# A three-layer float32 transformer kernel: order of the opening loads, the first normalisation, and the experts' scatter

## The reference, cut to what matters

```python
sc, scc = silu(c), silu(c_ctx)[None]
mod_x = (sc @ w_mod + b_mod).reshape(-1, 6, d)         # shift, scale, gate, shift, scale, gate
mod_c = (scc @ w_mod[:, :2 * d] + b_mod[:2 * d]).reshape(1, 2, d)
hx = rms_norm(x, g_mix) * (1 + mod_x[:, 1]) + mod_x[:, 0]
hc = rms_norm(ctx, g_mix) * (1 + mod_c[:, 1]) + mod_c[:, 0]
mx = hybrid_mixer(hx, hc, w_in, ...)                   # projections, retention, two attentions
x = x + mod_x[:, 2] * mx
h = rms_norm(x, g_ffn) * (1 + mod_x[:, 4]) + mod_x[:, 3]
# experts: each of 16 takes its 32 best tokens
aff = softmax(h @ w_router)
gate, idx = top_k(swapaxes(aff, 1, 2), 32)
xe = h[idx]
hid = silu(xe @ w_gate[e]) * (xe @ w_up[e])
ye = (hid @ w_down[e]) * gate[..., None]
x = x + mod_x[:, 5] * zeros_like(h).at[idx].add(ye)
# second block: layer 0 a sparse attention and an FFN, layer 1 a recurrent mixer and an FFN
```

## Time and profile before

| | us |
|---|---|
| median of three runs | 1835.61 (1831.35 to 1838.48) |
| profiled execution, its time | 1840.93 |
| its span in the trace | 1839.1 |
| busy in the span: TensorE / VectorE / ScalarE / GpSimd | 1531.6 / 783.6 / 579.6 / 20.5 |
| moved by DMA | 437.75 MB, mean 238 GB/s |

### The profile page before, as it was taken

One profiled execution on the slowest core, in us unless ns is written; L12 is line 12 of the kernel. 1 busy time (PEld: TensorE's weight loads), 2 busy tenths in 40 slices (PEclk: granted clock), 3 DMA queues, 4 the chain that ended last, 5 costly groups with the idle time before them and its releaser, 6 DMA issues.

```text
span 1839.1 us, 27187 instructions
## 1 busy us (share of the span) xinstructions
PE 1531.6 (83%) x11234; PEld 1153.2 (63%) x11234; DVE 783.6 (43%) x1178; ACT 579.6 (32%) x832; POOL 20.5 (1%) x21
## 2 busy tenths in 40 slices
PE   5899996789976566666666799988999989879999
PEld 1689884467952111111111699547999989779999
DVE  4333335356741000000001566544655366765553
ACT  3322124466321000000001332454433344733332
POOL 0000020000000000000000000000000000100000
PEclk9899998889968766767666898889999999889999
DMA  9665454512638999999999453663355535335540
GB/s 395 250 252 213 194 184 181 208 69 93 249 140 367 421 422 422 421 422 422 422 422 422 159 201 115 267 256 118 138 183 184 184 138 184 133 115 183 183 168 24
DMA packets 60417, 437.75 MB, mean 238 GB/s; under 512 B 6720, under 2 KB 6848, under 8 KB 7456
## 3 DMA queue, kind: packets, MB, share of 16 engines
q1 hardware_dynamic: 59328, 428.89, 59.8%
q10 hardware_dynamic: 720, 4.94, 0.6%
q0 software_dynamic: 272, 2.49, 0.4%
HBM read 435.25 MB, written 1.05 MB: 237 GB/s over the span
## 4 chain that ended last, share of the span: by engine, by line
PE 59%; DMA 20%; DVE 10%; SPq 4%; ACT 4%; issue 3%; DVEq 0%; ACTq 0%
PE bank L631 55%; DMA ring<-in_w 20%; SPq L551 4%; DVE ring_r L1566 2%; PE bank L635 2%; PE bank L972 1%; PE bank L951 1%; ACT ring_r L1264 1%; DVE arena L1863 1%; DVE norm_t L1529 1%; DVE arena L1985 0%; DVE arena L1687 0%; ACT arena L1413 0%; DVE H L1556 0%; DVE arena L1986 0%
## 5 line engine op out<-in xcount | busy, mean ns | idle before, releaser
L631 PE MATMUL bank<-H_r,ring_r 128*128 128x256 f32 x3488 | 509.9, 288 | 18.5 <-DVE H_r L1551 18.5
L631 PEld LDWEIGHTS bank<-H_r,ring_r 128*128 128x128 f32 x3488 | 464.5, 196 | 24.2 <-issue 22.6
L1566 DVE TENSOR_TENSOR ring_r<-ring,ring_r 128x2048 fp32r<-128x2048 f32 x136 | 313.7, 2308 | 239.5 <-ACT ring_r L1264 239.3
L631 PE MATMUL bank<-arena_r,ring_r 128*128 128x256 f32 x2776 | 396.7, 287 | 20.5 <-DVE ring_r L1566 16.6
L631 PEld LDWEIGHTS bank<-arena_r,ring_r 128*128 128x128 f32 x2776 | 368.4, 194 | 37.5 <-issue 21.4
L1264 ACT ACTIVATE ring_r<-ring 128x2048 fp32r<-128x2048 f32 x136 | 259.6, 1910 | 229.3 <-PE bank L631 164.6
L951 PE MATMUL bank<-ring,arena 128*32 128x512 f32 x1024 | 195.7, 857 | 112.3 <-DMA ring<-in_w 111.8
L951 PEld LDWEIGHTS bank<-ring,arena 128*32 128x32 f32 x1024 | 24.3, 126 | 267.3 <-DMA ring<-in_w 260.2
L1819 DVE TENSOR_TENSOR arena<-arena,bank 64x512 f32<-64x512 f32 x16 | 11.1, 691 | 290.9 <-ACT arena L1361 290.9
L1361 ACT ACTIVATE arena<-bank 64x512 f32<-64x512 f32 x16 | 9.4, 588 | 385.6 <-PE bank L951 385.6
L631 PE MATMUL bank<-ring,silu_c 128*32 128x512 f32 x576 | 81.3, 670 | 47.1 <-ACT norm_t L1355 21.6
(11 more groups left out here) (238 smaller groups left out, 1275.7 us busy)
## 6 DMA issues: line engine op xcount, KB each, us to landing
ring<-in_w SPq DMA_DIRECT2D x408, 1024.0 KB, 10.6
ring<-in_bias POOLq DMA_DIRECT2D x1, 2048.0 KB, 7.7
consts<-in_consts ACTq DMA_DIRECT2D x1, 1567.0 KB, 25.1
X<-in_x ACTq DMA_DIRECT2D x1, 1024.0 KB, 10.7
arena<-in_ctx ACTq DMA_DIRECT2D x1, 1024.0 KB, 15.2
arena<-in_decay ACTq DMA_DIRECT2D x1, 1024.0 KB, 19.7
out_t<-X SPq DMA_DIRECT2D x4, 256.0 KB, 2.0
wide<-in_wide POOLq DMA_DIRECT2D x1, 256.0 KB, 9.0
```

The lines of the kernel that those rows point to most:

```text
L631: i = nc.tensor.matmul(o, lhsT, rhs, start=start, stop=stop, skip_group_check=grouped)
L1566: v.tensor_tensor(r(lo), lo, r(hi), ALU.subtract).then_inc(lo_ready, 1)
```

## The change

- The loads of x and ctx move to the head of SyncE's queue, before the chunks. ScalarE's queue keeps cols and the first 256 columns of consts (`ident`, `ones`). The rest of consts, decay and `wide` are started by GpSimd after modulation block 0 is done.
- x's sum of squares comes before the first modulation chunk, ctx's (`sum_sq_c`) after the second; each then has its own square root and reciprocal, and VectorE multiplies x and ctx by their inverse norms at once (one 128x2048 instruction each).
- FILL_START is gone: the seven steps stay in the fill list. ("kr", 0)'s chunk is loaded seventh, before the last two of block 0, and is split before the row copy.
- Apply 0 is made of three parallel parts: ScalarE makes the rounded part with gain and shift in one instruction, GpSimd makes the full part, VectorE subtracts. All of x's tiles go first, then ctx's.
- The decay masks are made head by head between the projections ("decay_m", h).
- The experts' loop on TensorE is written out for 16 experts. The picks' weighting and transposes go into expert 0. The combine is cut into four `scatter` groups: experts 0 to 3 are accumulated into banks 3 to 6 after the gate and up products of expert 4, and so on; the last group is behind expert 15.

The core of the diff:

```diff
-    s = [("decay",)] + [("mod", 0, k) for k in range(5)] + [("sum_sq", 0)]
-    s += [("mod", 0, k) for k in range(5, KT)] + [("mod_row", 0), ("mod_out", 0)]
+    s = [("decay",), ("sum_sq", 0), ("mod", 0, 0), ("mod", 0, 1), ("sum_sq_c",)]
+    s += [("mod", 0, k) for k in range(2, KT)] + [("mod_row", 0), ("mod_out", 0)]
...
-    take(FILL_START)
-    for x in [("kr", 0), ("kr", 1), ("qr", 0), ("qr", 1), ("vr", 0), ("rot", "kr", 0), ("vr", 1), ("rot", "kr", 1),
+    for x in [("kr", 0), ("kr", 1), ("decay_m", 0), ("qr", 0), ("decay_m", 1), ("qr", 1), ("decay_m", 2),
+              ("vr", 0), ("rot", "kr", 0), ("decay_m", 3), ("vr", 1), ("rot", "kr", 1), ("decay_m", 4),
...
-    s += [("gather", k) for k in range(KT)] + [("pick_t", t) for t in range(2)]
+    s += [("gather", k) for k in range(KT)]
     s += [("experts",)]
...
+        if x[0] == "mod" and x[1] == 0 and x[2] == LATE_MOD:
+            keys.append(("kr", 0))
+        if x[0] in ONE_CHUNK and x != ("kr", 0):
             keys.append(x)
...
-        x = mine[1 - n] if len(mine) >= n - 1 else ("apply", 0) if c < FIRST_SECOND else ("sum_sq", 2)
+        x = mine[1 - n] if len(mine) >= n - 1 else ("mod_row", 0) if c < FIRST_SECOND else ("sum_sq", 2)
...
+            for t in range(2):
+                add(("pick_t", t), "act", SUM_BANK + 2 * t)
+            for p in range(4):
+                add(("combine", p), "dve", SUM_BANK + p)
...
+            sp_eng.dma_start(X[:, :, :], small["x"]).then_inc(x_landed, 16)
+            sp_eng.dma_start(ctx_in, small["ctx"]).then_inc(ctx_landed, 16)
             for c, s in enumerate(RING_USE[0][1]):
                 load(s, w[c])
             rounds(0)
...
+            eng.wait_ge(mod_done, 1)
+            eng.dma_start(consts[:, 256:], small["consts"][:, 256:]).then_inc(rest_landed, 16)
+            eng.dma_start(decay_in, small["decay"]).then_inc(decay_landed, 16)
             eng.dma_start(wide[:, :, :], small["wide"]).then_inc(wide_landed, 16)
+
+            eng.wait_ge(x_hat, 2)
+            eng.wait_ge(mod_a_ready, 2)
+            for c in range(2):
+                for k in range(KT):
+                    nc.gpsimd.tensor_scalar(h_0[:, k, c * T:(c + 1) * T], H[:, k, c * T:(c + 1) * T],
+                                            mod_a[:, 2 * c, k:k + 1], mod[:, k, c:c + 1], ALU.mult,
+                                            ALU.add).then_inc(h_scaled, 1)
 
...
-                            pe.wait_ge(h_split, 2 * k + 1 + c)
+                            pe.wait_ge(h_split, KT * c + k + 1)
...
-                owed[0] += 1
+                if blk or k < LATE_MOD:
+                    owed[0] += 1
...
+            def scatter(i):
+
+                pe.wait_ge(ye_taken, 4 * i + 5)
+                if i == 0:
+                    in_sbuf(("pick_t", 1))
+                for p in range(4):
+                    b = begin(("combine", p)) if i == 0 else bank[SUM_BANK + p]
+                    for half in range(2):
+                        n = 2 * p + half
+                        mm(b[:, half * T:(half + 1) * T], y_tok[:, i, n * P:(n + 1) * P], hot_t[:, i, :],
+                           i == 0 and half == 0, i == 3, job_done if i == 3 and half else None, grouped=True)
...
+                for e in range(EXPERTS):
+
+                    pe.wait_ge(x_cur_ready, e + 1)
+                    for k in range(KT):
+                        c = FIRST_EXPERT + 12 * e + k
+                        pe.wait_ge(landed[slot_of(c)], 16 * landed_count(c))
+                        for j in range(4):
+                            last = matmul(bank[0][32 * j:32 * j + 32, :], x_cur[:, k, :],
+                                          ring[:, k, 512 * j:512 * j + 512], start=k == 0, stop=k == KT - 1)
+                        last.then_inc(chunk_used if k < KT - 1 else gate_up_done, 1)
+
+                    if e == 0:
+                        turn_picks()
+                    if e and e % 4 == 0:
+                        scatter(e // 4 - 1)
+
+                    pe.wait_ge(hid_ready, e + 1)
...
+                    last.then_inc(down_done, 1)
+
+                    pe.wait_ge(down_done, e + 1)
+                    pe.sem_inc(chunk_used, 1)
+                scatter(3)
...
-            act.dma_start(X[:, :, :], small["x"]).then_inc(x_landed, 16)
-            act.dma_start(ctx_in, small["ctx"]).then_inc(ctx_landed, 16)
-            act.dma_start(decay_in, small["decay"]).then_inc(decay_landed, 16)
-            act.dma_start(consts[:, :], small["consts"]).then_inc(consts_landed, 16)
+            act.dma_start(consts[:, 0:256], small["consts"][:, 0:256]).then_inc(consts_landed, 16)
...
+                if ni == 0:
+                    act.wait_ge(x_hat, 2)
+                    act.wait_ge(mod_a_ready, 2)
+                    for c, hi in enumerate((hx_hi, hc_hi)):
+                        for k in range(KT):
+                            f(r(hi[:, k, :]), H[:, k, c * T:(c + 1) * T], ACT.Identity, bias=mod[:, k, c:c + 1],
+                              scale=mod_a[:, 2 * c, k:k + 1]).then_inc(h_ready, 1)
...
+                if ni == 0:
+                    v.tensor_tensor(H[:, :, 0:T], X[:, :, :], over(norm_t[:, 0, 0:T], KT), ALU.mult).then_inc(x_hat, 1)
...
+                    for c, hi in enumerate((hx_hi, hc_hi)):
+                        for k in range(KT):
+                            dve.wait_ge(h_ready, KT * c + k + 1)
+                            dve.wait_ge(h_scaled, KT * c + k + 1)
+                            v.tensor_tensor(r(H[:, k, c * T:(c + 1) * T]), h_0[:, k, c * T:(c + 1) * T], r(hi[:, k, :]),
+                                            ALU.subtract).then_inc(h_split, 1)
+                    return
...
+                weigh_picks()
```

More of the change, by code:

```diff
@@ L311, in plan_jobs @@
             add(("pick", "gate"), "act")
-        elif k == "pick_t":
-            add(x, "act")
         elif k == "cmp_s":
@@ L983, in step_experts @@
-                pe.wait_ge(ye_taken, EXPERTS + 1)
-            def step_combine(p):
-                b = begin(("combine", p))
-                if p == 0:
-                    in_sbuf(("pick_t", 1))
-                for i in range(2):
-                    n = 2 * p + i
-                    for j in range(4):
-                        mm(b[:, i * T:(i + 1) * T], y_tok[:, j, n * P:(n + 1) * P], hot_t[:, j, :], j == 0, j == 3,
-                           job_done if i == 1 and j == 3 else None)
+                                if kk == 0 and j == 3 and c:
+                                    last.then_inc(chunk_used, 1)
@@ L1515, in each, with step_sum_sq_c @@
                 return a.unsqueeze(2).to_broadcast([a.shape[0], a.shape[1], n])
-            dve.wait_ge(ctx_landed, 16)
-            v.tensor_tensor(sq_0[:, :, T:2 * T], ctx_in, ctx_in, ALU.mult).then_inc(sq_ctx, 1)
             def step_sum_sq(ni):
-                n = 2 * T if ni == 0 else T
                 b = job(("sum_sq", ni))
-                takes(v.tensor_scalar(norm_t[:, 0, 0:n], b[:, 0:n], 1.0 / D, EPS, ALU.mult, ALU.add), ("sum_sq", ni))
-                finish_std(ni)
-            def finish_std(ni):
-                n = 2 * T if ni == 0 else T
+                takes(v.tensor_scalar(norm_t[:, 0, 0:T], b[:, 0:T], 1.0 / D, EPS, ALU.mult, ALU.add), ("sum_sq", ni))
                 dve.wait_ge(std_ready, ni + 1)
-                link(v.reciprocal(norm_t[:, 0, 0:n], norm_t[:, 1, 0:n]))
+                link(v.reciprocal(norm_t[:, 0, 0:T], norm_t[:, 1, 0:T]))
+                if ni == 0:
+                    v.tensor_tensor(H[:, :, 0:T], X[:, :, :], over(norm_t[:, 0, 0:T], KT), ALU.mult).then_inc(x_hat, 1)
+            def step_sum_sq_c():
+                b = job(("sum_sq_c",))
+                at = slice(T, 2 * T)
+                takes(v.tensor_scalar(norm_t[:, 0, at], b[:, 0:T], 1.0 / D, EPS, ALU.mult, ALU.add), ("sum_sq_c",))
+                dve.wait_ge(std_c, 1)
+                link(v.reciprocal(norm_t[:, 0, at], norm_t[:, 1, at]))
+                v.tensor_tensor(H[:, :, at], ctx_in, over(norm_t[:, 0, at], KT), ALU.mult).then_inc(x_hat, 1)
             def step_apply(ni):
@@ L1554, in step_apply @@
+                    return
                 ahead = 2
-                for i, (k, x, gain, rstd, h, _, _) in enumerate(tiles):
-                    v.scalar_tensor_tensor(h[:, k, :], x[:, k, :], gain[:, k:k + 1], rstd, ALU.mult,
+                for k in range(KT):
+                    v.scalar_tensor_tensor(H[:, k, 0:T], X[:, k, :], mod_a[:, ni, k:k + 1], norm_t[:, 0, 0:T], ALU.mult,
                                            ALU.mult).then_inc(h_scaled, 1)
-                    if ni != 1 and i >= ahead:
-                        lower(i - ahead)
@@ L1560, in step_apply @@
-                for i in range(len(tiles) - ahead, len(tiles) if ni != 1 else 0):
-                    lower(i)
+                    if ni != 1 and k >= ahead:
+                        lower(k - ahead)
+                for k in range(KT - ahead, KT if ni != 1 else 0):
```

(13 more changed lines are left out.)

178 lines of the change are left out of this document (84 added, 94 removed).

## The result

The changed kernel takes **1809.68 us** (median of four runs, 1807.37 to 1812.57) against 1836.74 for the kernel before on the same chip: a ratio of **0.985**, with a 95% interval of 0.984 to 0.987. 1810 was predicted. The profiled execution took 1809.85 us, with a span of 1807.8, so 31.3 us of span are to be explained against the 25.7 of the sum; the medians differ by less (27.1), since the profiled execution of before lay 4.2 us over its median.

A forecast was written before the change was run, and what follows sets the result against it. Start and expert loop were taken as bound by bytes, the rest by TensorE and hand-overs. Terms -17.7 + 2.0 + 1.0 + 0 - 0.7 - 10.3 = -25.7 us on a 1839.1 span gave a 1810 median, range 1796 to 1824.

The forecast's parts named there:

- The opening: Start up to the first projection tile's end: fewer bytes ahead, 0.9 us per GpSimd tile, end near 52.5, gain 17.7 us.
- rival (a): First normalised input: GpSimd runs at 0.5 us a tile, giving 1804 us; chance 0.15.
- rival (c): First modulation block: TensorE, not the bytes, ends it, at 39.3 instead of 35.2, giving 1814 us; chance 0.04.
- The clock of the second tile: Second projection tile: TensorE, mostly idle before, starts it at the low clock, 24 matmuls at 0.22 instead of 0.13; +2.0 us.
- The projections: Projections before the attention: 24 instead of 23 fill chunks, +1.0 us; 2 us if one split is late.
- The attention stretch: Pairs 0 to 15 with 16 instead of 10 fill chunks: taken as 0, bounds -10 and +17 us.
- the spacing: Attention: four more filled pairs, at 11.7 against 7.5 us each, cost 17; the avoided row-copy wait returns 9.3: +8 us.
- Rival (b): Attention: fills cost what filled pairs cost, +12 to +17 us, 1822 to 1827; chance 0.22, with slow GpSimd another 0.05.
- The expert loop: Expert loop: transposes, copies and three early scatters fit into TensorE's idle time in the byte-bound loop; cost 0.
- Rival (d): Expert loop: fetches of written-out code stall TensorE by 10 us an expert; chance 0.04.
- The end: Combine after the last expert: 16 of 64 matmul records remain, 6.6 us instead of 16.92; -10.3 us.
- The start of the experts: Ahead of the expert matmuls: the wait for `hot_g` and 8 transposes go, some 0.3 stays; -0.7 us.

The follow-up runs named there:

- kr ninth: Changed kernel with kr 0's chunk loaded ninth, behind the whole first modulation block, and split just before the first normalised input; 1808.3 us, 0.985 of the kernel before.
- fills 36: Changed kernel with seven more fills ahead of the attention, behind qr, gr, qw and the first qn projections; 1820.9 us, 0.992 of the kernel before.

## Why the prediction came out right, point by point

**The opening** was to bring 17.7 us to the end of the first tile and brought 70.1 - 49.6 = 20.5 (the row at 69.92 of the earlier trace rows is the 49th matmul; the 48th ended at 70.08). The bytes were counted rightly, to 2 us: the last chunk was in by 31.4, not 33.3, and the block's matmuls ended at 33.3, not 35.2. The pace was 0.79 us a tile; 0.9 was chosen between 0.5 and 1.2. The reason given for it, that the two engines disturb each other, held: GpSimd by itself needs 0.54 (`kr ninth`), near what rival (a) has, and VectorE's turns bring it to 0.79. The pace of rival (a), and rival (c), with TensorE ending the block, are refuted by these rows.

**The clock of the second tile** was to cost 2.0 and cost nothing. Fed at 0.79 us a tile, TensorE was granted 2.4 GHz inside the first tile (windows of the tile and of what follows, columns as above):

```profile
37.00:50.00 13.00, 11.33 (x54) 9.45 (x55) 7.45 (x17) 9.03 (x16) 11.11 (x15) 0.78 0.60 248
50.00:61.00 11.00, 11.00 (x93) 9.43 (x92) 1.05 (x1) 0.78 (x2) 0.00 (x0) 1.00 0.31 106
```

It was not mostly idle, as I had put it: at 1.2 GHz three matmuls of 0.22 us or so fill a pace of 0.79, and its rows show no wait before the clock rose. It is also luck: in two of the seven traces with this pace (`kr ninth` and `fills 36`) the clock fell back at 48.4 and 49.1 us, and the second tile took 6.85 and 6.92 us instead of 5.76.

**The projections** were to cost 1.0, or 2 more for one late split. They cost 8.4. This is the step of the prediction that failed: 0.9 is the fill; 2.8 are three waits for splits, because the credits for an early kr 0 hold the next loads, which the working did not follow; 3.0 are the collision, which was in the earlier trace rows as the 4.75 us, used there for a pace and never asked where that addition would fall once everything ahead of it had moved. Some 1.7 stay without a row.

**The attention stretch** was taken at 0 and brought -6.3. The mechanism held: the 15.77 us went, with six fills more. It was mis-sized (before, with its one trace, 146.6; the new order 138.6 to 142.4 in nine); stepping the order by hand gave -3, the spacing +8. Rival (b), that fills cost what filled pairs cost, is refuted by `fills 36`: fewer fills there made it longer. This gain and the loss ahead of it nearly cancel (+2.1 against the +3.0 of the sum, clock included), which is why the total came out so close.

**The expert loop** was taken at 0 and cost 2.9. Rival (d) named the right thing, fetches of written-out code beside full DMA engines, but looked for it at TensorE, as a stall of 10 us an expert. It came as late chunks, which this byte-bound stretch could not hide.

**The end** was to bring 10.3 and brought 11.7. The accumulations fell from 16.92 to 3.72 us, 13.2 less, as the 16 left ran at 2.4 GHz; counted from their start VectorE begins the next norm 12.6 earlier, and 1.0 of that is lost behind it, where the next sum of squares took 6.12 us instead of 5.14. The start of the experts, -0.7 foreseen, gave 1.6 over its whole stretch; TensorE's wait there is 1.61 where a wait of 1.01 and the transposes stood.

The parts of the sum were off by +7.4 (projections), -6.3 (attention), +2.9 (loop), -2.8 (opening), -2.0 (clock), -1.4 (end) and -0.9 us (way to the experts), and by -2.5 in the part with no change. The median of 1810 owes as much to their cancelling as to the working.

## What to carry to other kernels

A two-input VectorE instruction that started behind a GpSimd instruction waited for its end here, and a GpSimd instruction behind VectorE's did too. So cut a long GpSimd instruction that may fall beside VectorE's work into pieces, and ask, with every change ahead of it, where it will fall now. Work that is slid under waits has to be followed in order on every engine that serves it, a small copy behind a long chain being worth more than the matmuls; and in a byte-bound loop every late chunk counts in full, here 2 to 3 us that came with written-out code.

## What had not been expected of the hardware

- VectorE's split of 128x2048 stood still for the whole of a GpSimd addition (10.31 us instead of 2.29; its end 2.15 us behind GpSimd's in all nine traces), and lost only 0.42 us when the addition was cut in 16. A GpSimd instruction of 0.54 us that fell beside such a split took 3.08.
- GpSimd and VectorE sharing a two-step job took 0.79 us a tile of 128x256, VectorE alone 0.66, though GpSimd's step by itself takes 0.54.
- 15 packets of instructions (0.25 MB) among full DMA queues went with chunks late by 2.3 to 3.1 us in all, in slips of 0.5 to 1.6 us, each 2.2 to 4.2 us behind the start of a packet.
- A TensorE fed a step of three matmuls every 0.79 us was granted 2.4 GHz on the way (0.41, then 0.28 us a record), and kept it with waits of 0.17 us at each step; in two of seven traces with that pace it fell back once (second tile 6.9 us instead of 5.8).
